# Attention in a hybrid encoder layer: values as the stationary operand, inverse row sums through DRAM

## What is computed

```python
h = rms_norm(x, g); z = h @ w_in          # q/k/v attention, q/k/v/gate retention, two merge gates
s = einsum('bnqhd,bnkhd->bnhqk', qc, kb) * dh**-0.5 + bias     # chunk band: causal by chunk of 64
o = einsum('bnhqk,bnkhd->bnqhd', softmax(s), vb)               # 8 heads of 64
ret = retention(rotary(qr), rotary(kr), vr, state)             # 4 heads of 128
m = sigmoid(ga) * (o @ w_attn_out) + sigmoid(gb) * (norm(ret) * silu(gr) @ w_ret_out)
x = x + rms_norm(m @ w_o); x = x + rms_norm(relu(rms_norm(x) @ w_up)**2 @ w_down)
```

## Time and profile before

| | us |
|---|---|
| median of three runs | 876.26 |
| the profiled execution | 877.14 |
| its span in the trace | 875.3 |
| TensorE matmul busy | 865.2 |
| VectorE busy | 501.2 |
| ScalarE busy | 314.5 |
| GpSimd (POOL) busy | 9.6 |

### The profile page before, as it was taken

The page is one execution under the profiler, slowest core; times in us unless marked ns, Lnnn a source line. Parts: engine busy times, 40 slices in busy tenths (PEclk is TensorE's granted clock), DMA queues, the critical chain, the costliest instruction groups (busy, mean ns, idle before and its releaser), DMA issues.

```text
span 875.3 us, 16857 instructions
## 1 busy us (share of the span) xinstructions
PE 865.2 (99%) x6900; PEld 850.7 (97%) x6900; DVE 501.2 (57%) x867; ACT 314.5 (36%) x483; POOL 9.6 (1%) x13
## 2 busy tenths in 40 slices
PE   8999999999999999999999999999999999999996
PEld 8999999999999999999999999999999999999996
DVE  5333687787788567676437756654333443244345
ACT  6211455455441111254446442124312331134342
POOL 1000000000000000000100000000000000000000
PEclk9999999999999999999999999999999999999998
DMA  9333212223222312121241122322223312332202
GB/s 303 99 97 96 74 49 85 71 63 120 74 98 60 99 55 95 57 86 62 93 145 49 50 97 97 96 72 72 97 97 96 96 63 81 96 97 96 94 5 103
DMA packets 78011, 77.32 MB, mean 88 GB/s; under 512 B 2976, under 2 KB 75312, under 8 KB 77968
## 3 DMA queue, kind: packets, MB, share of 16 engines
q1 hardware_dynamic: 68784, 70.39, 24.9%
q10 hardware_dynamic: 8544, 4.15, 1.8%
q0 software_dynamic: 640, 2.17, 0.7%
HBM read 71.70 MB, written 4.99 MB: 88 GB/s over the span
## 4 chain that ended last, share of the span: by engine, by line
PE 97%; DVE 1%; DMA 1%; ACT 0%; issue 0%; DVEq 0%
PE acc L829 75%; PE wk L853 3%; PE wk L829 3%; PE wk L999 3%; PE acc L904 1%; PE wk L1120 1%; PE acc L1120 1%; PE acc L1121 1%; PE wk L1121 1%; PE wk L1122 1%; PE acc L1122 1%; PE wk L961 1%; PE wk L960 1%; PE wk L1066 1%; PE wk L1075 1%; DMA ident_sb<-in_ident 1%
## 5 line engine op out<-in xcount | busy, mean ns | idle before, releaser
L451 ACT ACTIVATE w_hi<-w_raw 128x1024 fp32r<-128x1024 f32 x115 | 122.1, 1062 | 425.0 <-PE acc L829 403.2
L829 PE MATMUL acc<-act_hi,w_hi 128*128 128x272 f32 x1184 | 248.6, 291 | 0.0
L829 PE MATMUL acc<-act_hi,w_lo 128*128 128x272 f32 x1184 | 245.1, 288 | 0.0
L829 PE MATMUL acc<-act_lo,w_hi 128*128 128x272 f32 x1184 | 244.2, 288 | 0.0
L829 PEld LDWEIGHTS acc<-act_hi,w_hi 128*128 128x128 f32 x1184 | 186.0, 188 | 3.7 <-issue 0.8
L829 PEld LDWEIGHTS acc<-act_lo,w_hi 128*128 128x128 f32 x1184 | 186.0, 188 | 0.0
L829 PEld LDWEIGHTS acc<-act_hi,w_lo 128*128 128x128 f32 x1184 | 184.9, 189 | 0.0
L1304 DVE TENSOR_TENSOR w_lo<-w_raw,w_hi 128x1024 fp32r<-128x1024 f32 x115 | 140.7, 1223 | 37.7 <-ACT w_hi L451 37.5
L829 PE MATMUL acc<-mid_hi,w_hi 128*128 128x272 f32 x544 | 112.2, 287 | 0.0
L829 PE MATMUL acc<-mid_hi,w_lo 128*128 128x272 f32 x544 | 111.8, 288 | 0.0
L829 PE MATMUL acc<-mid_lo,w_hi 128*128 128x272 f32 x544 | 111.7, 287 | 0.0
(11 more groups left out here) (285 smaller groups left out, 1011.2 us busy)
## 6 DMA issues: line engine op xcount, KB each, us to landing
w_raw<-in_w_in SPq DMA_DIRECT2D x43, 512.0 KB, 4.4
w_raw<-in_w_ff_up SPq DMA_DIRECT2D x32, 512.0 KB, 4.7
w_raw<-in_w_ff_down SPq DMA_DIRECT2D x32, 512.0 KB, 4.0
w_raw<-in_w_o SPq DMA_DIRECT2D x8, 512.0 KB, 4.0
x_nat<-in_x_prompt SPq DMA_DIRECT2D x4, 512.0 KB, 5.7
w_raw<-in_w_attn_out SPq DMA_DIRECT2D x4, 512.0 KB, 4.0
w_raw<-in_w_ret_out SPq DMA_DIRECT2D x4, 512.0 KB, 5.7
k_cache<-in_cache_attn_k SPq DMA_DIRECT2D x1, 1024.0 KB, 10.1
```

Source lines behind the costliest of these rows:

```text
L451: act.activation(w_hi[:, v % 2], w_raw[:, v // 2, :, P * (v % 2):P * (v % 2) + P], ACT.Copy).then_inc(hi_ready, 1)
L829: ins = pe.matmul(dst[:, n, 0:HALF], w[:, k, :], h[:, k, HALF * n:HALF * n + HALF], start=begin, stop=end)
```

## The change

- `probs_times_v`: the values become the stationary operand, 128 columns wide: `v_stack` holds, for each block of 128 keys, the high parts of both heads' values with the low parts between them, so that a slice of it is one head's high and low part. The transposed probabilities, split into `p_hi` (ScalarE) and `p_lo` (VectorE), move, up to 512 columns at once. The product comes out feature-major, with one half of the rows from the values' high and one from their low parts; ScalarE copies one half (`low_rows`), VectorE adds both into `z` (`att_add`). The sample rows stay token-major and get one transpose (`sample_transposed`, `sample_back`).
- The inverse row sums now lie on the wrong axis. POOL stores them to DRAM and loads them back spread over 64 partitions, head by head, and VectorE multiplies during the next pair (`normalise`), for the last pair ahead of the fifth gate tile's rest.
- The second head's transposes and product move into tile 0 of the next pair (the first gate tile for the last pair), the first head's into the end of tile 2 and tile 3 (`second_head`, `first_head`, `between_heads`). The loops over pairs are written out.
- Keys and values are read from `z`, without copies; blocks of keys are turned by VectorE at three places (`keys_blocks`).
- ScalarE's queue, instead of POOL's, issues the loads of `rope`, `decay` and `state_in`. VectorE rotates the keys of head 0 around the last head's work, and the queries of head 0 after the first gate tile.
- Fillers: nine instead of seven ahead of the x tiles, none between them.

```diff
         # gpsimd
-            pool.wait_ge(scores_mm, 2 * PAIRS)
-            pool.dma_start(rope[:], a["rope"]).then_inc(ret_const_in, 16)
...
+            for h in range(AH):
+                pool.wait_ge(inv_ready, h + 1)
+                pool.dma_start(inv_dram[h].rearrange("(t p) -> p t", p=P), row_inv[:, 0:4], allow_slow_non_contiguous=True).then_inc(inv_out, 16)
+                if h % 2 == 0 and h:
+                    pool.wait_ge(attT_ready, h // 2)
+                pool.wait_ge(inv_out, 16 * h + 16)
+                pool.dma_start(inv_spread[AD * (h % 2):AD * (h % 2) + AD, :], bass.AP(inv_dram.tensor, SEQ * h, [[0, AD], [1, SEQ]]))\
+                    .then_inc(inv_in, 16)
         # scalar
+            def probs_high(i, e):
+                for b, (col, n) in enumerate(PT_BANKS):
+                    act.wait_ge(pT_mm, 6 * i + 3 * e + b + 1)
+                    act.activation(p_hi[:, col:col + n], wk[:, col:col + n], ACT.Copy).then_inc(p_hi_ready, 1)
+            def low_rows(i, e):
+                rows, others = slice(AD * e, AD * e + AD), slice(AD - AD * e, 2 * AD - AD * e)
+                act.wait_ge(pv_mm, 4 * i + 2 * e + 1)
+                act.activation(att_low[rows, :], wk[others, PV_COL:PV_COL + SEQ], ACT.Copy).then_inc(att_low_ready, 1)
...
+            act.wait_ge(scores_mm, 2 * PAIRS)
+            act.dma_start(rope[:], a["rope"]).then_inc(rope_in, 16)
+            act.dma_start(decay[:], a["decay"]).then_inc(ret_const_in, 16)
+            act.dma_start(state_in[:], a["state_retention"].rearrange("h d e -> d h e")).then_inc(ret_const_in, 16)
+            exps(PAIRS - 1, 1)
+            split_ahead(G_RET + PAIRS - 1, 3)
+            probs_high(PAIRS - 1, 1)
+            low_rows(PAIRS - 1, 1)
...
-            act.wait_ge(attT_ready, PAIRS + 1)
+            act.wait_ge(att_added, 2 * PAIRS)
             evacuated(act, G_RET + PAIRS - 1, 3)
             act.activation(gate_sig[:], z[:, Z_RG:Z_RG + RH, :], ACT.Sigmoid).then_inc(gate_sig_ready, 1)
         # tensor
-            warm_up(wk[:, 1920:2048], 7)
+            warm_up(wk[:, 1920:2048], 9)
...
-                if t in (1, 2):
-                    warm_up(wk[:, 1920:2048], t)
...
             def probs_times_v(i, e):
...
+                for b in (0, 1, 3, 2):
+                    if b < 3:
+                        pe.wait_ge(p_hi_ready, 3 * h + b + 1)
+                        pe.wait_ge(p_lo_ready, 3 * h + b + 1)
+                    v = v_stack[:, b, 2 * e:2 * e + 2, :].rearrange("p n c -> p (n c)")
+                    cols = slice(PT_COL[b], PT_COL[b] + SEQ - P * b)
+                    pe.matmul(wk[:, PV_COL + P * b:PV_COL + SEQ], v, p_hi[:, cols], start=(b == 0), stop=False)
+                    ins = pe.matmul(wk[:, PV_COL + P * b:PV_COL + SEQ], v, p_lo[:, cols], start=False, stop=(b == 2))
...
-                pe.wait_ge(att_nat_ready, 2 * i + 2)
-                for t, (s, n) in enumerate(TILES):
-                    ins = tr(wk[:, s:s + n], att_nat[0:n, t, :])
-                ins.then_inc(att_tr, 1)
...
+                between = {0: second_head(PAIRS - 1), 1: sample_transposed(PAIRS - 1, rv_nat_ready, 1)}.get(u)
         # vector, a pair
+                if i:
+                    masked_max(i - 1, 1)
+                    to_z(g - 1, 3, Z_RQ + 4 * i - 1)
+                queries_low(i)
+                if i:
+                    split_ahead(g - 1, 3)
+                    row_inverse(i - 1, 1)
+                    probs_low(i - 1, 1)
                 keys_low(i, 0)
+                if i:
+                    att_add(i - 1, 1)
...
+                values_low(i)
+                keys_blocks(i, range(2, 13))
                 to_z(g, 1, Z_RQ + 4 * i + 1)
+                split_ahead(g, 1)
                 masked_max(i, 0)
+                keys_low(i, 1)
+                row_inverse(i, 0)
+                probs_low(i, 0)
                 to_z(g, 2, Z_RQ + 4 * i + 2)
+                if i:
+                    normalise(i - 1)
+                att_add(i, 0)
                 split_ahead(g, 2)
+                keys_blocks(i, range(13, 16)).then_inc(k_nat_ready, 1)
...
-            rotate_keys(0)
-            rotate_queries(0)
+            rotate_cross(Z_RK, 0)
+            split_ahead(G_GATE - 1, 3)
+            row_inverse(PAIRS - 1, 1)
+            probs_low(PAIRS - 1, 1)
+            rotate_add(Z_RK, 0, k_rotated)
+            att_add(PAIRS - 1, 1)
```

More of the change, by code:

```diff
@@ L1003, in probs_times_v @@
                 ins.then_inc(pv_mm, 1)
+                out = wk[0:DEC, PV_SAMPLE:PV_SAMPLE + AD]
+                for b in range(4):
+                    pe.matmul(out, p_sample[:, DEC * b:DEC * b + DEC], v_cache[:, b, AD * e:AD * e + AD], start=(b == 0), stop=False)
+                pe.matmul(out, p_sample[0:DEC, 4 * DEC:5 * DEC], v_nat[0:DEC, 4, AD * e:AD * e + AD], start=False, stop=True).then_inc(pv_mm, 1)
             def to_natural(src, col):
```

380 lines of the change are left out of this document (219 added, 161 removed).

## The result

The kernel before took 876.67 us (876.16 to 877.86, six runs), the changed one **871.70 us** (871.18 to 873.04, six runs): a ratio of 0.9944, 95% interval 0.9931 to 0.9957, or 5.0 us less (3.8 to 6.0). The forecast was 865.9, with a range up to 871.6. The direction was right, less than half of the gain came, and the time lies just outside the range. The profiled execution took 871.64 us, its span is 869.8.

What follows compares the result with a forecast made beforehand. TensorE, busy 99% of the span, was taken to bound the kernel. 12.2 us less work plus 0.9 at the front, minus 1.4 of waits and 1.3 at the retention's entrance, gave 10.4, so 865.9 us (range 862.8 to 871.6).

Steps and rivals of the forecast that it cites:

- product of probabilities and values: TensorE, prompt part: eight instructions instead of 20, 2.38 us a head falling to 1.24, 9.1 gained over eight heads.
- transposes of the probabilities: TensorE in attention: same number but back to back, 0.1 us gained a head, 0.8 in all.
- waits of second heads, first heads: TensorE in attention: second heads wait 0.15 us at the product, first heads 0.2 at the transposes; 1.4 lost together.
- retention constants by ScalarE: End of attention: three issues moved to ScalarE's queue cost 0; 3 us if the rotary tables landed at the slowest 8.0.
- entrance of the retention: Retention's first scores: TensorE waits 1.3 us for rotated queries behind the last head's addition and sigmoid; between 0 and 2.5.
- front: Kernel start: changed fillers let x tiles be transposed sooner, 0.9 us gained, with the clock rising no later.
- Rival 5: Product in attention: the values' weight loads show in full, 0.96 us a head, 7.7 in all; 873.6 us, chance 0.05.
- rival 3: Front: without fillers the clock stays at 1.2 GHz until the first products, losing 4.8 and 0.9; 871.6 us, chance 0.06.
- Inverse row sums, 0: POOL's queue: 16 small DMAs, two in a row taking 16 us, fit the some 24 available; cost 0.
- Rival 4: Attention: the inverse sums' round trip makes VectorE wait from 24 us on; at 28, 882 us in all, chance 0.05.
- Rival 2: Attention: copies too slow, last bank 0.5 to 1 us later a head; 868.5 to 872.5 us, chance 0.14.
- Rival 1: Whole kernel: all copies covered, no new waits, front 1.25, 13.4 us gained; 862.9 us, chance 0.13.

Runs made afterwards that it cites:

- the kernel with early tables: Changed kernel with rotary tables loaded one pair earlier, other constants issued behind the last high parts, first queries rotated earlier, first heads' maxima before the weight split: 866.63 us.
- the rotation's 1.6: Changed kernel with VectorE's rotation of the first retention keys moved behind the last head's subtractions: 871.83 us, ratio 0.9952 to the kernel before.
- with the maxima first: Changed kernel with each pair's first-head row maxima taken ahead of the second tile's weight split: 871.48 us, ratio 0.9948 to the kernel before.

## Why the prediction was wrong

The forecast's sum was 10.4. Its parts for attention came to 9.5; the profiles show 4.2. Term by term, in us (the measured ones are distances from start to start, added up over both profiles):

| term | forecast | measured |
|---|---|---|
| product of probabilities and values | 9.1 | 7.8 |
| transposes back | 2.3 | 2.2, less 0.4 in the slices ahead of the sample's |
| transposes of the probabilities | 0.8 | -0.9, and -0.3 in the slices behind |
| waits of second heads, first heads | -0.6, -0.8 | 0, -1.3 |
| retention constants by ScalarE | 0 | -2.0 |
| entrance of the retention | -1.3 | -1.0 |
| front | 0.9 | 1.4 between the two profiles, but 0.0 (-0.8 to 0.8) between the medians |

In the kernel with early tables, where nothing waits, the product comes to 8.1, and the transposes of the probabilities with the slices behind them to -0.9. The differences to the table, some 0.7, are paid by the first instructions behind a wait (a first transpose takes 0.167 in place of 0.109, the last product 1.63 in place of 1.37). So the waits cost 4.9 in all, where the forecast had 2.7, and the work saved on TensorE is 9.1, where it had 12.2.

- **The step that failed most: "The rotary tables landed 4.0 after issue; VectorE asks for them 5.1 after the scores. ... I take their own row, 0."** The bound of 3 was named and the wrong end taken. VectorE did ask 4.9 after the scores. But the tables were ready 7.6 after them, 2.3 for an issue behind the key stores and 5.3 for the landing. I had counted the three issues that were moved, not the two stores that they were moved *behind*, nor that ScalarE's queue can stand still. The other half of the step, "the last exponentials wait for the maxima until 4.4 anyway: 0", failed with it: they began 3.7 after the scores and ended at 6.5, 0.8 later than forecast. What the runs showed in place of the 0: a wait of 2.0 at the last product, of which 1.3 came back with the tables issued first and 1.6 by POOL's queue; the last 0.3 hung on ScalarE's late exponentials too, and all of it was gone once the tables were loaded early and no issue stood ahead of the exponentials.
- **Transposes back to back, 0.8 gained:** refuted by cutting them again. I read the cost of a group from its total, whose last member hides 0.08 in the next group's first. At the upper clock a transpose of 128 rows costs 0.109 in every group seen here, short or long. What the change adds is that the small transposes are followed by slices (first matmul 0.23) where they ran into the product before.
- **The product, 1.24 a head:** 1.37. The rule of the Trainium skill ("TensorE: Matmul & The Clock Gate", section "LDWEIGHTS") gave an estimate of 1.27, nearer. The trace agrees in part: the two narrow ones take 0.06 and 0.11, 0.17 together against 0.21 by the rule. What neither had is 0.05 and 0.09 more at the two of 256 columns that follow. Rival 5, the loads in full, is out.
- **First and second heads:** the mechanism for the first heads was right (the weight split ahead of the maxima; taking it away took the wait away), 0.2 a head as forecast in three pairs and 0.7 in the first, where VectorE's key blocks still ran when the tile ended. The second heads do not wait at the product; only the last one's transposes come 0.1 late.
- **The entrance** was right, chain and size (1.3 forecast, 0.8 in the list and 1.0 by distance).
- **The front:** I noted that the profiled execution was 0.9 above the median, then took a difference measured in it off the median. The clock rose no later, as forecast, but it need not have been the filled gap: with the gap there the transposes went from 0.21 to 0.11 apart (the granted clock's step from 1.2 to 2.4 GHz) at 5.4, 7.3 and 10.7 us in three profiles, with nine fillers at 7.1 in one, and in the changed kernel's profile they stood 0.11 apart from the first tile on. With seven fillers and none between, TensorE had nothing but transposes from 4.86 on when they sped up at 7.3, and the third tile's eight took 1.04, where the eight at the lower level took 1.80. The sentence of the Trainium skill that spoke against it (same page, "Part 4: PE-mode transpose") does not hold here, and rival 3 is out; that its 871.6 lies beside the measured time is chance.
- **Inverse row sums, 0:** right. Rival 4 had 16 for the round trip; it took 14.5. **Keys, 0:** right in three pairs; in the first the blocks outlast the tile by about 1 and cost some 0.5 of the first head's 0.7.
- **Rival 2** had the time in its range, but not the mechanism: the copies are not too slow, one transfer was too late. **Rival 1** named a state that the kernel with early tables reaches, no waits, but not its size: 9.1 in place of 12.2 on TensorE.

Without the wait of 2.0 the time would have been some 869.7 by this account, inside the range. The remaining misses are three readings of rows (transposes, narrow products, the front); together they weigh more than the tables, 3.1 on TensorE and 0.9 at the front.

## What to carry over

When a DMA issue is moved to another queue, write down what stands ahead of it there and allow its landing the slowest row, not its own row from a quieter place; better, find the tables a place that is free earlier, since what is gained elsewhere falls onto the next late thing (0.8 of the maxima's 1.4 onto the tables, the rotation's 1.6 onto the entrance). A group's cost includes what the next group's first instruction pays, and a difference seen in one profile is checked against that execution's place among the runs.

## What was not expected of the hardware

- A pause of TensorE of 1.6 to 1.9 us at the last product was followed in some executions by 6.8 us at a granted clock of 0.50 (1.2 GHz in place of 2.4), and in others by nothing (the changed kernel: 1.9 and no fall in its profile; with the maxima first: 2.7 and none). Where it fell, 3.4 us were lost beyond the wait. That the pause brings the fall is likely, not shown: the fall stands behind it in both profiles that have one, but its length does not decide.
- The same 544 KB landed in 4.0 us from POOL's queue before, in 4.3 to 6.9 in this place from either queue, and in 7.1 and 7.6 a pair earlier. No run shows why.
- A lone transpose of 32 rows costs TensorE 0.36 with its surroundings (0.09 in the slice ahead, 0.17, 0.10 behind), three times one of 128 rows.
- ScalarE's queue stood 1.7 to 3.8 us in its second issue at the end of the last pair, in every profile of the changed kernel and its variants. The traffic of the changed kernel in that stretch (231 to 235 us; queue, packets, MB, share of 16 engines) shows a load of program code in flight:

```profile
q10 hardware_dynamic: 500, 0.25, 22.1%
q8 instruction: 1, 0.02, 5.2%
```

One packet with 5.2% of 16 engines' 4 us took 3.3 us (231.3 to 234.7, where the issue ends at 234.8). The loops over pairs are written out now, and no such pause stands at the key stores before. In all fourteen profiles of the changed kernel and its variants the long issue ends 0.2 to 0.4 after that packet, which took 2.8 to 4.1. But not every load does this: in the changed kernel an issue at 138.3, within a load of 6.1, took its usual 0.5. That the load is the cause is argued from the times alone; no run takes it away.
